# The sum of squares of four RMS norms: eight accumulated products with ones, or seven additions and one product

## What is computed

```
def rms_norm(x, g, eps=NORM_EPS):
    xf = x.astype(jnp.float32)
    y = xf * lax.rsqrt(jnp.mean(xf * xf, axis=-1, keepdims=True) + eps)
    return (y * g.astype(jnp.float32)).astype(x.dtype)
...
for layer in range(DEPTH):
    if layer < N_A_LAYERS:
        h = rms_norm(x, g_mix[layer])            # norm 0
        x = x + rwkv7_time_mix(h, ...)
    else:
        k_sh, v_sh = shared_kv(x, kv_g, kv_w, k_norm_g, pos)
        h = rms_norm(x, g_mix[layer])            # norm 2
        x = x + diff_attention(h, k_sh, v_sh, pos, ...)
    h = rms_norm(x, g_ffn[layer])                # norm 1, norm 3
    x = x + swiglu_ffn(h, ffn_w_gu[layer], ffn_w_down[layer])
```

## Time and profile before

| | us |
|---|---|
| median of 3 runs | 2186.15 |
| the three runs | 2186.15, 2180.63, 2186.2 |
| profiled execution: span from first to last instruction | 2180.4 |
| PE busy | 1976.5 (91%) |
| DVE busy | 792.0 (36%) |
| ACT busy | 759.7 (35%) |
| POOL busy | 756.0 (35%) |
| mean granted TensorE clock | 0.956 |

### The profile page before, as it was taken

How to read it: one execution, slowest core, us unless ns; L and a number is a source line. 1 busy time by engine, 2 the same in 40 slices (tenths; PEclk the granted TensorE clock), 3 DMA queues, 4 the chain that set the end, 5 groups by cost and what they waited for, 6 DMA issues and landing times.

```text
span 2180.4 us, 35345 instructions
## 1 busy us (share of the span) xinstructions
PE 1976.5 (91%) x14896; PEld 1577.9 (72%) x14896; DVE 792.0 (36%) x1269; ACT 759.7 (35%) x1047; POOL 756.0 (35%) x656
## 2 busy tenths in 40 slices
PE   5997997765999999989999899999999999979897
PEld 3665867664778888866677478888887886768767
DVE  5586334444332221026576532222002123233333
ACT  6766233333332222132256433222112423242232
POOL 3353300002444444434331144444444533334532
PEclk8998989997999999999999899999999999989988
DMA  5111100001233333221211023333232311122211
GB/s 157 58 44 47 37 3 4 4 23 59 58 97 96 96 96 99 94 87 59 77 40 40 20 77 97 96 96 96 92 101 78 97 59 39 45 96 66 70 41 57
DMA packets 190132, 147.06 MB, mean 67 GB/s; under 512 B 6826, under 2 KB 188289, under 8 KB 190004
## 3 DMA queue, kind: packets, MB, share of 16 engines
q1 hardware_dynamic: 190004, 145.18, 21.6%
HBM read 143.07 MB, written 2.10 MB: 67 GB/s over the span
## 4 chain that ended last, share of the span: by engine, by line
PE 76%; DVE 7%; ACT 6%; issue 6%; POOL 4%; DMA 1%; SPq 0%; DVEq 0%; ACTq 0%; POOLq 0%
PE psum L2531 20%; PE psum L2533 19%; PE psum L2532 19%; POOL w_lo L1135 4%; PE psum L2701 4%; ACT w_hi L1256 2%; DVE X_lo L1818 1%; PE psum L2974 1%; PE psum L2912 1%; PE psum L2987 1%; PE psum L2903 1%; PE psum L2875 1%; PE psum L2537 1%; PE psum L3083 1%; PE psum L2878 1%
## 5 line engine op out<-in xcount | busy, mean ns | idle before, releaser
L1135 POOL TENSOR_TENSOR w_lo<-weight_raw,w_hi 128x256 fp32r<-128x256 f32 (+4 forms) x616 | 718.1, 1197 | 1204.5 <-ACT w_hi L1256 1204.4
L2531 PE MATMUL psum<-X_hi,w_hi 128*128 128x512 f32 x1400 | 585.0, 418 | 37.1 <-DVE X_lo L1818 26.2
L2533 PE MATMUL psum<-X_hi,w_lo 128*128 128x512 f32 x1400 | 553.5, 395 | 0.0
L2532 PE MATMUL psum<-X_lo,w_hi 128*128 128x512 f32 x1400 | 553.4, 395 | 0.0
L1256 ACT ACTIVATE w_hi<-weight_raw 128x2048 fp32r<-128x2048 f32 (+2 forms) x134 | 249.2, 1860 | 354.5 <-PE psum L2533 333.7
L2531 PEld LDWEIGHTS psum<-X_hi,w_hi 128*128 128x128 f32 x1400 | 267.2, 191 | 135.4 <-issue 66.2
L2532 PEld LDWEIGHTS psum<-X_lo,w_hi 128*128 128x128 f32 x1400 | 267.7, 191 | 63.1 <-issue 12.1
L2533 PEld LDWEIGHTS psum<-X_hi,w_lo 128*128 128x128 f32 x1400 | 267.2, 191 | 57.9
L2531 PE MATMUL psum<-w_hi,X_hi 128*128 128x256 f32 x640 | 191.6, 299 | 13.2 <-DVE X_lo L1818 10.9
L2532 PE MATMUL psum<-w_lo,X_hi 128*128 128x256 f32 x640 | 185.0, 289 | 0.0
L2533 PE MATMUL psum<-w_hi,X_lo 128*128 128x256 f32 x640 | 184.8, 289 | 0.0
(11 more groups left out here) (457 smaller groups left out, 2455.9 us busy)
## 6 DMA issues: line engine op xcount, KB each, us to landing
weight_raw<-in_ffn_w_gu SPq DMA_DIRECT2D x88, 512.0 KB, 5.0
weight_raw<-in_l_w_in SPq DMA_DIRECT2D x45, 512.0 KB, 4.7
weight_raw<-in_ffn_w_down SPq DMA_DIRECT2D x40, 512.0 KB, 3.6
weight_raw<-in_kv_w SPq DMA_DIRECT2D x16, 512.0 KB, 4.1
weight_raw<-in_l_w_out SPq DMA_DIRECT2D x16, 512.0 KB, 4.0
weight_raw<-in_rw_w_k SPq DMA_DIRECT2D x8, 512.0 KB, 6.8
weight_raw<-in_rw_w_r SPq DMA_DIRECT2D x8, 512.0 KB, 4.0
weight_raw<-in_rw_w_v SPq DMA_DIRECT2D x8, 512.0 KB, 4.0
```

What stands on the lines that cost most here:

```text
L1135: ins = pool.tensor_tensor(l, r, h.bitcast(F32), ALU.subtract)
L2531: pe.matmul(ps, wh, xh, start=start, stop=False, skip_group_check=True)
L2532: pe.matmul(ps, wh, xl, start=False, stop=False, skip_group_check=True)
L2533: return pe.matmul(ps, wl, xh, start=False, stop=stop, skip_group_check=True)
```

## The change

The eight products with ones per norm become one. DVE adds the squares up in `rt` as ACT delivers them (seven additions of 128 x 512, `add_square`), and PE multiplies that sum by ones once (`norm_sum`). In norm 0 the additions stand ahead of everything DVE does. In norms 1 to 3 addition k - 1 stands behind the `X_lo` of tile k - 1, for k from 2 on, and the seventh at the end. The single product with ones stands in the second step of the next product, ahead of its k group 1. ACT's square of tile k (k from 2 on) now waits for addition k - 1 (`sq_added` at 7 i + k - 1), where it waited for the ones of tile k - 2.

```
-                        act.wait_ge(sq_used, 7 * i + k - 1)
+                        act.wait_ge(sq_added, 7 * i + k - 1)
                     act.activation(square_buffer(i)[:, k % 2, :], x[:, k, :], ACT.Square).then_inc(sq_ready, 1)
...
+            def add_square(i, k):
+
+                dve.wait_ge(sq_ready, 8 * i + k + 1)
+                if k > 1:
+                    dve.wait_ge(sq_added, 7 * i + k - 1)
+                buf = square_buffer(i)
+                dve.tensor_tensor(rt[:, :], buf[:, 0, :] if k == 1 else rt[:, :], buf[:, k % 2, :], ALU.add
+                                  ).then_inc(sq_added, 1)
...
                     if k:
                         x_low1(v, k - 1)
+                    if k >= 2:
+                        add_square(i, k - 1)
                 x_low1(v, KT - 1)
+                add_square(i, KT - 1)
                 norm_scale(i)
...
+            for k in range(1, KT):
+                add_square(0, k)
             wait_done(dve, ("xt", KT - 1))
             dve.memset(h_sb[:, :, 0:1], 0.0)
             norm_scale(0)
...
-                features(s0, v, check=False, parts=norm_beside(1 + 2 * layer))
+                features(s0, v, check=False)
                 pe.wait_ge(step_d, PL.taken[s0 + 1][1] - 2)
-                features(s0 + 1, check=False)
+                features(s0 + 1, check=False, parts=norm_beside(1 + 2 * layer))
...
-            def norm_part(i, k):
-
-                if k == 0:
-                    begin(("rms", i))
-                pe.wait_ge(sq_ready, 8 * i + k + 1)
-                pe.matmul(bank(6), c_("ones"), square_buffer(i)[:, k % 2, :], start=k == 0, stop=k == KT - 1
-                          ).then_inc(sq_used if k < KT - 1 else job_done, 1)
+            def norm_sum(i):
+
+                pe.wait_ge(sq_added, 7 * i + 7)
+                b = begin(("rms", i))
+                pe.matmul(bank(b), c_("ones"), rt[:, :], start=True, stop=True).then_inc(job_done, 1)
 
             def norm_beside(i):
 
                 def part(k):
-                    if k:
-                        norm_part(i, k - 1)
-                    if k == KT - 1:
-                        norm_part(i, k)
+                    if k == 1:
+                        norm_sum(i)
                 return part
...
-            for k in range(KT):
-                norm_part(0, k)
+            norm_sum(0)
...
+            def query_part(n):
+                if n >= KT:
+                    norm_beside(2)(n - KT)
+                qk_part(n)
+
             for i in range(4):
-                features(PL.first["q"] + i, XV["qin"] if i == 0 else None,
-                         parts=norm_beside(2) if i == 0 else lambda k: qk_part(8 * i + k))
+                features(PL.first["q"] + i, XV["qin"] if i == 0 else None, parts=lambda k: query_part(8 * i + k))
```

More of the change, by code:

```diff
@@ L806, in build @@
         xhi_ready, xlo_ready = sem("xhi_ready"), sem("xlo_ready")
-        sq_ready, sq_used = sem("sq_ready"), sem("sq_used")
+        sq_ready, sq_added = sem("sq_ready"), sem("sq_added")
         heads_ready = sem("heads_ready")
```

## The result

The changed kernel takes 2187.49 us, the kernel before 2179.34 us, each the median of 20 runs. The ratio is 1.0038 with an interval of 1.0025 to 1.0051: slower by 8.2 us, just beyond the 0.3% (6.6 us) that the prediction named as the edge of what can be told. The forecast was +1.6 on a base of 2186.15, the median of three runs. Those three lay high: over 20 runs the base is 6.8 lower. So the forecast of 2187.7 met the time by luck: 6.8 too much for the base and 6.6 too little for the change cancelled. Only the second is worth learning from.

The account below looks back on a forecast made before the run. It took the bound to be chains PE waits for (`X_lo`, `w_lo`, the rope table), not PE's work. Norm 0 +3.7, norms 1 and 3 -0.2 each, norm 2 -1.7 gave +1.6 on 2186.15: 2187.7 us, range 2180 to 2195.

Parts of the forecast that it names:

- That 24.6 us less work on PE bring nothing: Whole kernel: 28 fewer products with ones at 0.88 us take 24.6 us from PE, yet no time is won.
- Rival A: Whole kernel: PE is the bound after all, all 28 products count; 2161.5 us, or 2171.4 with norm 0 as forecast; 3%.
- Norm 0, +3.7: Norm 0: ACT's squares and DVE's additions alternate at 1.40 us a round, so the root comes 3.7 us later, uncovered.
- Norms 1 and 3, -0.2 each: Norms 1 and 3: third step 1.9 us earlier, less 1.7 for the clock; bounds -3.4 to +1.5 each.
- the second step's start: Norm 1, same pattern in norm 3: the second step starts at 596.35 instead of 602.26, 5.9 us earlier.
- the clock: Norms 1 and 3, behind the third step's wait: PE granted 0.57 of the clock for 4.0 us, costing 1.7 us.
- The wait itself: Norms 1 and 3: PE waits about 4.2 us before the third step, where it waited 0.93.
- the first step: Norm 1: the first gu step should be about 11.5 us long in the trace after.
- Norm 2, -1.7: Norm 2: rope table lands earlier, the root 0.7 us later ends last, PE's rotation 1.7 us earlier; bounds -4 to +0.5.
- Rival C: Norms 1 and 3: DVE's additions hold POOL up, 3.1 us more in each, so 2194 us; 20%.
- B: All norms: waits cost no clock and slot 1 comes early; -6.6 us in all, 2179.5 us; 15%.
- D: Norms 1 and 3: additions keep the products waiting, first step no shorter than 17.1 us; +5.6 each, 2199 us; 5%.

Follow-up runs that it names:

- e2: The changed kernel with ACT's square of tile k waiting for addition max(1, k - 2), not k - 1: 2179.2 us, ratio 1.0003 against the kernel before.
- e9c: The changed kernel again, the same program in another series of runs: 2188.16 us, ratio 1.0034 against the kernel before.
- e1: The changed kernel with norm 0 as before (eight products with ones), additions only in norms 1 to 3: 2181.93 us, ratio 1.0020 against the kernel before.
- e6b: The changed kernel with ten products of constants on PE ahead of norm 0's product with ones, into an unused bank; a single profiled run, 2184.21 us.
- e3: The changed kernel with ACT's `high` of slot 2 ahead of the first hidden tile in both feed-forward layers: 2169.86 us, ratio 0.9963 against the kernel before.
- e4: The kernel before with only ACT's `high` of slot 2 moved ahead of the first hidden tile: 2173.51 us, ratio 0.9979 against the kernel before.
- e5b: The changed kernel with norms 1 to 3's product with ones in the next product's first step, before its last k group: 2165.7 us, ratio 0.9935 against before.
- e7b: The changed kernel with old norm 0, slot 2's `high` earlier; in norm 2 earlier product with ones, small DVE operations and rope table: 2161.71 us, ratio 0.9917 against before.
- e8c: The kernel before with norm 0 alone changed (seven additions, one product with ones): 2183.8 us, ratio 1.0020 against the kernel before.
- e10c: The kernel before with `high` of slot 2 ahead of the first hidden tile and the rope table loaded earlier: 2173.23 us, ratio 0.9961 against before.

## Why the prediction was right and wrong

- **That 24.6 us less work on PE bring nothing**: right, and it came out as a loss. Rival A is out; with A the time would have been 2155 or 2165 on the base of 20 runs.
- **Norm 0, +3.7**: measured +4.2 from the first square, +3.9 in the pair of stages. The alternation is there; a round is 1.45 instead of 1.40 (two hops of 0.13 together, one of them, 0.10, above its bound of 0.08), and PE's product took 2.07 instead of 1.91, at half clock as priced. The choice of that row was right. The reason given, that with two buffers the engines cannot overlap, was wrong: e2 has two buffers and they do.
- **Norms 1 and 3, -0.2 each**: wrong in two terms, not in the mechanism. The first is the second step's start: forecast 5.9 earlier, measured 5.07. POOL needed 7.80 for slot 1 instead of 7.2. What fell beside it was just what had been reckoned, one scaling, two `X_lo` and two additions (rows below: 0.97 and four of 1.22 or 1.23), and these five turns took 5.56 from 589.98 on, for 0.88 + 4 x 1.14 = 5.44 forecast. But five turns and three pieces of 0.70 alone are 7.54 by the prediction's own prices; the 7.2 that I put down was 0.3 short of them, and the other 0.3 is turns and pieces a little longer than priced. All that hangs on it moved by 0.8 to 0.9: the root 1.0 earlier instead of 1.9, the third step 1.07 instead of 1.9. The second is the clock: 5.2 us at half level, 2.6 us of work, where the earlier trace rows had given 4.0 at 0.57, 1.7. One row of another place was taken for a price that differs from execution to execution. Together -1.07 + 2.6 = +1.5 instead of -0.2, by the stage +1.4 (in the second execution +1.2). The wait itself, forecast 4.2, was 4.01, and the first step, forecast 11.5 long, lasted from 584.43 to 596.10, 11.67.

```profile
589.98 0.97 DVE L1854 TENSOR_SCALAR xf<-x,pv 128x512 f32<-128x512 f32 x1
590.87 1.23 DVE L1818 TENSOR_TENSOR X_lo<-xf,X_hi 128x512 fp32r<-128x512 f32 x1
592.02 1.23 DVE L1836 TENSOR_TENSOR rt<-rt,pt 128x512 f32<-128x512 f32 x1
593.16 1.23 DVE L1818 TENSOR_TENSOR X_lo<-xf,X_hi 128x512 fp32r<-128x512 f32 x1
594.32 1.22 DVE L1836 TENSOR_TENSOR rt<-rt,pt 128x512 f32<-128x512 f32 x1
```

- **Norm 3** repeats it (a wait of 3.99 before its third step), but behind it the lower level lasted 3.4 us in this execution and in e2, which is the 1.7 that was forecast, and 5.3 us in e9c, e1 and e6b, where it had begun during the wait. Norms 2 and 3 together are -0.7, where -1.9 was forecast.
- **Norm 2, -1.7**: measured -1.04. The table came in time and the later root ended last, as worked out. The size is off since the root came 0.9 later, not 0.7, and since DVE's six small operations took 0.4 longer (2.05 from 980.41 to 982.46, for 1.6 before).
- **The sum**: forecast +1.6, by the stages (norm 0 from its first square) +4.9 and +4.6, by the runs +8.2 and +6.9. The terms missed by 0.5 (norm 0), 1.6 (norm 1) and 1.2 (norms 2 and 3), all to the same side, together 3.3.
- **What stays open**: some 2 to 3 us more in the runs than in the stages. The lower edges of the two intervals are +5.4 and +4.1, for stages' sums of +4.9 and +4.6, so the second allows its sum and the first just does not. Nor is a rest of this size special to the changed kernel. Medians minus stages (cut in the same way), each against before, are +3.6 in e1, +0.2 in e2, +1.0 in e3, -2.0 in e4, -7.8 in e5b, +0.5 in e7b, -1.5 in e8c and -2.5 in e10c. So the rest may be scatter; no run here decides it. The granted clock points somewhere: its mean over the runs is 0.948 for the changed kernel (0.947 in e9c) and 0.954 to 0.956 before, which is about 30 us more at the lower level in a whole execution. The profiles place about 14 of these ahead of the first product, where PE idles but for the product with ones (its 0.95 is in norm 0's price), 7 in norm 1, 3 in norms 2 and 3. The remaining 6 would be 3 us of work and would lie where the code is the same. Why a stretch with the same code should be granted less isn't shown, and single profiles, in which that stretch spends from 67 to 95 us at the lower level, can't show it.
- **Rival C** was half right. The additions do hold POOL up beside slot 0 (8.25 instead of 7.53), but `w_lo` was still ready at 584.05, before the first step could start at 584.43. The delay came one slot later, as part of the 7.80, and cost a second step that starts later, not a first one. Rivals B and D did not come: no clock for free, and the second step did start 5 us earlier.
- **The chances**: most of it stood on "within 0.3%", and the result lies just outside, on the slower side, which had 23%. The bounds of norms 1 and 3 reached to +1.5 each. I had treated them as if they were as likely on the side of a gain; each term had its next rival on the side of a loss.

## What to carry to other kernels

Before work is taken from the busiest engine, find its next wait downstream and what that wait's chain starts from: here the work taken away came back as a wait for a chain that hung on the very product that had been moved back, and two small changes of order (e3, e5b), tried one at a time, turned +0.4% into -0.4% and -0.65%. A wait that a change creates on PE is to be priced with the clock behind it, and from more than one row of another place. Two engines that hand a tile back and forth should be checked for the index they wait on: one looser index (e2) gave back 3.25 of 4.2 us.

## What the runs showed of the hardware

- A wait of PE of 4.0 us was followed by 3.4 to 5.3 us of work at the lower level, in the same kernel and at the same place (norm 3); a wait of 1.35 or 1.53 by none (e5b, and the second step in norm 1). In between it is open: the wait of 2.40 before the last stage's first product brought the lower level for 3.4 us in eleven of the twelve profiled executions of this document, and not at all in e5b, though PE had been busy ahead of it in all. It is a matter of the execution too, not only of the wait.
- A product with ones in f32 lasts 1.02 us at the full level, 1.12 where PE had been idle for 1.5 to 2.6 us (e5b, e6b), and 2.07, at half the clock, after 7.88 or 11.13 (e2, the changed kernel).
- The length of a very small DVE operation depends on where it falls. The first of the six in norm 2, with one element per partition, took 0.56 in the changed kernel (rows below, its timeline, DVE and POOL) and 0.16 in the kernel before, though POOL was subtracting beside it in both. It may have had to wait for the rest of a piece, of which POOL's eight there take 0.69 each; no run here separates this.

```profile
980.41 0.56 DVE L2220 TENSOR_TENSOR col<-col 128x1 f32<-128x1 f32 x1
...
978.86 5.51 POOL L1135 TENSOR_TENSOR w_lo<-weight_raw,w_hi 128x256 fp32r<-128x256 f32 x8 [5.24 <-ACT w_hi L1256]
```

- The same program of this length spreads over 0.8% (2175.7 to 2193.1 in 20 runs), and the medians of the kernel before in different series lie between 2177.9 and 2181.3, where three runs gave 2186.15. A median of three can be off here by as much as the effect that is looked for.
